# Expert rows of a decoder layer gathered by a list made on chip, in place of a scatter and block loads

## The chip, the cores and the metric

The kernel runs on one core of one Trainium2 chip. The time is device microseconds of one execution, and the figure compared is the median of the runs. All data is float32.

## The reference, cut to what matters

One layer of a decoder: 512 tokens of width 1024, an attention part, then a mixture of 16 experts with a gated residual. The expert part is what the change touches:

```python
def grouped_moe(u, w_router, w1, w3, w2):
    xt = u.reshape(B * T, D)                                  # 512 x 1024
    aff = softmax(xt @ w_router)                              # 16 experts in 4 groups
    g_sel = argmax(group_score)                               # best group by its two best affinities
    top_w, top_i = top_k(where(in_group, aff, -1.0), 2)       # two experts of that group
    ...
    for e in range(16):
        h = silu(xt @ w1[e]) * (xt @ w3[e])                   # 1024 -> 512
        y = y + gate[:, e:e + 1] * (h @ w2[e])                # 512 -> 1024
```

Each token needs only its two experts, so the kernel computes 1024 rows in all.

## The kernel before, in words

Everything up to the router is left as it is. Its last part, L1189 to L1208, projects the attention output in pieces and makes `norm_x`, the normalised rows: ACT's `x_hat(i)` (L703) writes a tile of 128 tokens and counts `r_xh`; with them the columns are already in the order in which the four 256-wide parts of a row are wanted.

**Routing.** DVE finds the two experts of each token (L1224 to L1244), TensorE counts tokens per expert with small products (L1721), and DVE turns the counts into blocks of `BT` = 32 rows, at least `MIN_BLOCKS` = 2 for each expert, and into `posf`, the place of each of a token's two rows among all blocks (L1249 to L1257). For the inputs of the reference the experts take 3, 2, 3, 2, 2, 3, 2, 3, 3, 2, 2, 3, 3, 4, 3 and 2 blocks, 42 in all.

**Rows to blocks.** The DRAM buffer `xs` (`expert_rows`) is zeroed early (L454), and once `idx` is there GpSimd scatters `norm_x` into it with eight indirect DMAs (L833), 128 rows of 4 KB each. The rows of a block are then loaded from it, 32 partitions by 1024, by ACT's queue (`xg_load`, L726) into one of two buffers, and DVE copies them to `xg` (`rows_in`, L1286). The first `NH` = 3 blocks do without: DVE writes a table `pick` of ones and zeros (L1261), and TensorE multiplies it with `norm_x` (`pick_rows`, L1734), which gives each block as 128 partitions by 256, four parts of a row over each other.

**A block.** TensorE's `stage_of(g, ...)` (L1784) is `inner` (L1766: 64 matmul instructions, the two first matrices), `xg_T` (L1756: eight transposes of the next block's rows), and `outer` (L1777: 32 instructions, the third matrix, for the block before). ACT does the SiLU (L730), DVE the product with it (L1315), the scaling of the transposed rows (L1296, L1299), the copy of the block after next (L1286), a transpose (L1303) and the output scaling (`rows_out`, L1308). `inner(g)` waits at its last eighth for `m_cp`, the copy of block g + 1; the next `inner` waits for `m_xv`, its scaled rows. GpSimd stores the block's output rows into `xs` (`store_rows`, L843).

**Weights.** SP's queue loads three matrices of 2 MB for each expert (`load_matrix`, L468). There are four buffers for the pairs of first matrices and three for the third ones. The order is written out by hand (L474 to L513): for expert e the third matrix of e + 3 after the last block's `outer`, then the two first ones of e + 4. At the start experts 0 and 1 and two matrices of expert 2 are there early; (3, 1), (3, 0) and (2, 0), named as (expert, matrix), wait for the scatter (L490 to L500), since `norm_x` and the routing tables lie where they go. (4, 0) and (4, 1) follow when the third block's `inner` is done.

**End.** After the last `outer` the last rows are stored, GpSimd gathers both rows of each token from `xs` (L855), DVE weighs and adds them (L1369, L1374), and SP stores the output (L518).

Of the kernel before, what the change touches and what calls it, by code (L numbers as in the profile page):

```python
# [13 lines left out]
P = 128  # L14
# [34 lines left out]
NH = 3  # L49
N_SCAT = 6  # L50
# [3 lines left out]
N_ROWS = -(-(MAXB + 2) * BT // P) * P  # L54


def decoder_layer(nc, x, c, w_router, ada_w, ada_b, norm1_g, norm2_g, w_in, w_out, nsa_q_gain, nsa_k_gain,
# [6 lines left out]
    with ctx:  # L64
# [42 lines left out]
        def view(at, *shape):  # L107
# [3 lines left out]
            v = att[:, at[0]:at[0] + n]  # L111
# [7 lines left out]
        at = [0]  # L119
# [42 lines left out]
        at = [5120]  # L162
        aff, first, second, gate, cand, aff2 = [view(at, TT, NE) for _ in range(6)]
        both = att[:, 5120 + TT * NE:5120 + 3 * TT * NE].rearrange("p (b x) -> p b x", b=2)
# [10 lines left out]
        assert at[0] <= 6144  # L175
# [3 lines left out]
        zeros_f = sb("zeros_f", [P, 2 * P])  # L179
# [4 lines left out]
        xg = rowbuf[0:BT, 0:D]  # L184
        xg_in = [rowbuf[(1 + n) * BT:(2 + n) * BT, 0:D] for n in range(2)]
# [21 lines left out]
        first_xg = zeros_f[:, :]  # L207
        place = sb("place", [P, NH * BT])
# [128 lines left out]
        s_rows = sem("s_rows")  # L337
        s_ys = [sem(f"s_ys{n}") for n in range(2)]
        s_scat = sem("s_scat")
        s_scat_end = sem("s_scat_end")  # L340
# [69 lines left out]
        def _(sp):  # L410
# [72 lines left out]
            sp.dma_start(mod_rows_col[:], mod_dram.rearrange("(s a) (b k) -> (a b) s k", s=2, k=KD)).then_inc(s_mr, 16)  # L483
            for i in range(TT - 1):
# [37 lines left out]
        def _(act):  # L522
# [209 lines left out]
            def block_of_rows(g, n):  # L732
                silu_of(g)
                act.wait_ge(m_cp, g + 3)
                xg_load(g + 4, n)

            for g in range(2):
                silu_of(g)
            act.wait_ge(s_scat, 16 * N_SCAT)
            act.wait_ge(s_scat_end, 16 * (2 * TT - N_SCAT))  # L740
            xg_load(3, 1)
            xg_load(4, 0)
            act.wait_ge(m_cp, 4)
            xg_load(5, 1)
# [9 lines left out]
            act.wait_ge(s_xg[1], pairs * 16)  # L754
            nc.scalar.activation(cond_e[:], cond_e[:], ACT.Copy)

        @block.gpsimd
        def _(pool):
# [9 lines left out]
            nc.gpsimd.iota(place[:], pattern=[[1, NH * BT]], base=0, channel_multiplier=0, allow_small_or_imprecise_dtypes=True)  # L768
# [44 lines left out]
            nc.gpsimd.memset(zeros_f[:], 0.0).then_inc(t_const, 1)  # L813
# [14 lines left out]
            pool.wait_ge(s_rows, 16 * N_ZERO)  # L828
            pool.wait_ge(r_xh, TT)
# [1009 lines left out]
```

## Time and profile before

| What | Value |
|---|---|
| median of 3 runs | 689.77 us (687.86 to 694.4) |
| the profiled execution's own time | 687.71 us |
| its span in the profile | 686.0 us |
| TensorE busy | 605.6 us, 88% |
| DVE, ACT, GpSimd busy | 58%, 23%, 10% |
| mean granted TensorE clock | 0.96 |

The span is what the profile shows from the first to the last instruction; 1.7 us of the execution lie around it. Busy times are shares of that span. A matmul's end is modelled, and in the last two thirds of the expert part TensorE is busy nearly without a gap, while the sixteen DMA engines are too.

### The profile page before, as it was taken

To read this page: it belongs to the slowest core of one execution; us is meant where nothing else is said; L and a number is where in the kernel's file an instruction comes from. 1 tells how busy PE (TensorE), PEld (TensorE's weight loads), DVE (VectorE), ACT (ScalarE), POOL (GpSimd) and SP (SyncE) were. 2 spreads that over 40 slices of the span, in tenths; PEclk is the share of its full clock that TensorE was granted. 3 is DMA by queue.
4 is the path that set the end of the run, shared out by engine and by line. 5 is a ranking of instruction groups with operands and counts; after the bars stand their busy time and mean duration, and the time that the engine had idled before them with its cause. 6 is when DMAs were issued, how large, how long until landed. Compare 5 with 4: busy or idle time off the path is not lost.

```text
span 686.0 us, 15994 instructions
## 1 busy us (share of the span) xinstructions
PE 605.6 (88%) x6493; PEld 378.1 (55%) x6493; DVE 400.6 (58%) x1018; ACT 157.6 (23%) x405; POOL 71.2 (10%) x121
## 2 busy tenths in 40 slices
PE   0999999998898899779999989999999789999940
PEld 0654474577666566555447646666655445656620
DVE  4746709324489999962335645666655544666636
ACT  5201000103566667851335000000000000000000
POOL 6010000008100000000000400000000000000022
PEclk9999999999899999999999989999999989999975
DMA  8995936144699400019403899999999999999828
GB/s 312 389 400 210 358 117 245 62 126 132 204 332 216 140 1 1 1 57 427 193 32 149 342 360 387 390 387 379 380 380 391 391 406 399 376 370 383 302 62 330
DMA packets 43973, 180.39 MB, mean 263 GB/s; under 512 B 5714, under 2 KB 22698, under 8 KB 35722
## 3 DMA queue, kind: packets, MB, share of 16 engines
q1 hardware_dynamic: 35328, 157.11, 62.1%
q0 software_dynamic: 4352, 13.91, 5.5%
q10 hardware_dynamic: 4236, 8.55, 3.7%
q8 instruction: 44, 0.72, 0.4%
q14 instruction: 13, 0.11, 0.0%
HBM read 156.74 MB, written 22.81 MB: 262 GB/s over the span
## 4 chain that ended last, share of the span: by engine, by line
PE 36%; DMA 17%; DVE 1%; POOL 1%; issue 1%; POOLq 0%; DVEq 0%; ACT 0%
DMA pool_sb<-in_moe_w 14%; PE score L1766 13%; PE score L1632 8%; PE score L1777 8%; PE bank L1756 2%; PE bank L1386 1%; DMA pool_sb<-expert_rows,idx 1%; DMA pool_sb<-expert_rows 1%; POOL pool_sb L855 1%; PE bank L1734 1%; PE bank L1670 1%; DVE gate_row L1308 0%; PE bank L1681 0%; DMA expert_rows<-gate_row 0%; PE bank L1577 0%
## 5 line engine op out<-in xcount | busy, mean ns | idle before, releaser
L1766 PE MATMUL score<-pool_sb 128*32 128x256 f32 x2688 | 157.8, 388 | 10.8 <-DMA pool_sb<-in_moe_w 8.4
L1766 PEld LDWEIGHTS score<-pool_sb 128*32 128x32 f32 x2688 | 89.0, 112 | 72.5 <-issue 14.7
L1411 PE MATMUL bank<-pool_sb 128*128 128x512 f32 (+2 forms) x256 | 84.6, 491 | 0.7 <-DVE pool_sb L932 0.5
L1777 PE MATMUL score<-pool_sb 128*32 128x256 f32 x1312 | 81.0, 388 | 1.7 <-DMA pool_sb<-in_moe_w 1.4
L730 ACT ACTIVATE pool_sb<-score 128x128 f32<-128x128 f32 x41 | 11.4, 278 | 259.7 <-PE score L1766 250.0
L1308 DVE TENSOR_TENSOR gate_row<-score,gate_part 32x256 f32<-32x256 f32 x164 | 67.9, 414 | 3.7 <-PE score L1777 1.4
L1411 PEld LDWEIGHTS bank<-pool_sb 128*128 128x128 f32 x256 | 48.5, 190 | 36.1 <-issue 31.6
L1315 DVE TENSOR_TENSOR pool_sb<-pool_sb,score 128x128 f32<-128x128 f32 x42 | 15.9, 378 | 88.2 <-ACT pool_sb L730 86.4
L1632 PE MATMUL score<-pool_sb 128*128 128x512 f32 (+1 forms) x144 | 57.1, 549 | 0.0
L1777 PEld LDWEIGHTS score<-pool_sb 128*32 128x32 f32 x1312 | 39.1, 111 | 25.5 <-DMA pool_sb<-in_moe_w 2.0
L636 ACT ACTIVATE pool_sb<-pool_sb,nmax 128x128 f32<-128x128 f32 (+2 forms) x96 | 50.0, 526 | 4.6 <-DVE nmax L1036 4.5
L843 POOL DMA_DIRECT2D expert_rows<-gate_row x42 | 20.7, 492 | 248.6 <-DVE gate_row L1308 248.6
L1554 PE MATMUL bank<-ident,pool_sb 128*128 128x128 f32 x216 | 29.7, 280 | 15.6 <-DVE pool_sb L1068 15.4
L1632 PEld LDWEIGHTS score<-pool_sb 128*128 128x128 f32 x144 | 26.6, 190 | 24.9 <-issue 24.2
L1554 PEld LDWEIGHTS bank<-ident,pool_sb 128*128 128x128 f32 x216 | 23.1, 141 | 29.8 <-DVE pool_sb L1068 28.3
L925 DVE SCALAR_TENSOR_TENSOR pool_sb<-pool_sb,cond 128x2048 f32<-128x2048 f32 x16 | 37.5, 2347 | 1.5 <-DMA pool_sb<-in_ada_w 0.7
L1541 PE MATMUL score<-pool_sb 64*128 64x256 f32 (+3 forms) x192 | 32.9, 458 | 0.9 <-ACT pool_sb L621 0.9
L1036 DVE CUSTOM_DVE_ANT_0 pool_sb<-score,pool_sb 128x128 f32<-128x128 f32 (+2 forms) x64 | 27.9, 487 | 9.3 <-PE score L1541 9.1
L1756 PEld LDWEIGHTS bank<-ident,pool_sb 32*128 32x128 f32 x328 | 23.8, 139 | 17.1 <-issue 17.1
L1286 DVE COPY pool_sb<-pool_sb 32x1024 f32<-32x1024 f32 x40 | 27.3, 681 | 6.8 <-DMA pool_sb<-expert_rows 5.6
L1068 DVE TENSOR_SCALAR pool_sb<-pool_sb,fac 128x128 f32<-128x128 f32 (+2 forms) x96 | 29.4, 366 | 1.0
L1577 PE MATMUL bank<-pool_sb 128*64 128x128 f32 x432 | 29.6, 279 | 0.0
(274 smaller groups left out, 692.1 us busy)
## 6 DMA issues: line engine op xcount, KB each, us to landing
pool_sb<-in_moe_w SPq DMA_DIRECT2D x48, 2048.0 KB, 30.6
pool_sb<-in_ada_w SPq DMA_DIRECT2D x16, 1024.0 KB, 7.0
expert_rows<-zeros_f SPq DMA_DIRECT2D x17, 512.0 KB, 6.3
expert_rows<-gate_row POOLq DMA_DIRECT2D x42, 128.0 KB, 7.0
pool_sb<-expert_rows ACTq DMA_DIRECT2D x41, 128.0 KB, 6.9
pool_sb<-in_ada_w SPq DMA_DIRECT2D x8, 640.0 KB, 12.6
pool_sb<-in_w_out SPq DMA_DIRECT2D x4, 1024.0 KB, 16.5
pool_sb<-in_ada_w SPq DMA_DIRECT2D x8, 384.0 KB, 8.6
```

The costliest lines, as they stand in the source:

```text
L636: m = nc.scalar.activation(p, p, ACT.Exp, scale=-1.0, bias=nmax[:, u % 3, b, n:n + 1], accum_out=sums[:, u % 3, b, n:n + 1])
L925: nc.vector.scalar_tensor_tensor(out=acc[:, g % 2, :], in0=stage[:, n % 3, :], scalar=cond[:, k:k + 1], in1=acc[:, g % 2, :], op0=ALU.mult ...
L1068: m = nc.vector.tensor_scalar(p, p, fac[:, b, n:n + 1], None, ALU.mult)
L1308: m = nc.vector.tensor_tensor(y[:, h * DN:(h + 1) * DN], banks[bank][rows, 0:DN], gate2_part[rows, :], ALU.mult)
L1411: m = nc.tensor.matmul(pj_bank(g, i)[:, 0:n], featT[:, k, i * P:(i + 1) * P], w_stage[:, g % 3, k, 0:n], start=(k == 0), stop=(k == KD - 1))
L1541: m = nc.tensor.matmul(banks[2 * (u % 2) + b][:, off:off + w], qT[half, slot_of(t), q * P:(q + 1) * P], kT[half, r, k0:k0 + w], start=True ...
L1554: m = nc.tensor.transpose(banks[4 + b][:, at0:at0 + P], probs[:, u % 3, b, at0:at0 + P], ident[:])
L1577: m = nc.tensor.matmul(O[b * DH:(b + 1) * DH, q * P:(q + 1) * P], proj[:, k0 // P + n, V_COL[r] + b * DH:V_COL[r] + (b + 1) * DH], probsT[ ...
L1632: m = nc.tensor.matmul(banks[2 * (j % 2) + g][:, 0:n], featT[:, 4 * g + k, i * P:(i + 1) * P], w_out_sb[:, 4 * g + k, c0:c0 + n], start=(k ...
L1756: m = nc.tensor.transpose(banks[4][:, k * BT:(k + 1) * BT], xg[:, k * P:(k + 1) * P], ident[0:BT, 0:BT])
L1766: mm = nc.tensor.matmul(banks[0][h * BT:(h + 1) * BT, 0:2 * HB], xgT[:, k, :], w[:, :, h, :], start=(k == 0), stop=(k == KD - 1))
L1777: mm = nc.tensor.matmul(y[h * BT:(h + 1) * BT, 0:DN], h_of[:, c * BT:(c + 1) * BT], exp_w2[e % 3][:, c, h * DN:(h + 1) * DN], start=(c == ...
```

## The change

The scatter, the loads of blocks and their eight transposes go. `norm_x` is stored to DRAM in token order (`xh_dram`, four DMAs of 512 KB). A list `row_list`, 128 rows by one column for each block, is made on chip: for each place in a block it says which 1 KB quarter row of `xh_dram` each partition takes. It comes from a product of two one-hot tables (`rows_hot` times the token number, `blocks_hot`). GpSimd then gathers each block from the third on with one indirect DMA of 128 rows of 1 KB, in the layout 128 by 256 that so far only the first blocks had, so that all blocks need two transposes. `NH` is 2. The routing tables move to a tile of their own, and (3, 0) waits for the router's products alone.

```diff
-NH = 3
-N_SCAT = 6
+NH = 2
+N_LIST = MAXB + 3
...
-        xg = rowbuf[0:BT, 0:D]
-        xg_in = [rowbuf[(1 + n) * BT:(2 + n) * BT, 0:D] for n in range(2)]
+        xg = rowbuf[:, 0:DN]
+        xg_in = [rowbuf[:, (1 + n) * DN:(2 + n) * DN] for n in range(2)]
...
+        routing = sb("routing", [P, 576])
+        xh_tiles = xh_dram.rearrange("(i p) d -> p i d", p=P)
+        xh_parts = xh_dram.rearrange("t (c n) -> (t c) n", c=NT)
...
@@ block.sync @@
             for i in range(TT - 1):
                 store_x2(i)
+                store_x_hat(sp, i)
             sp.wait_ge(o_pj, NS)
             load_matrix(1, 0)
+            store_x2(TT - 1)
             load_matrix(1, 1)
-            store_x2(TT - 1)
-            sp.wait_ge(s_scat, 16 * N_SCAT)
+            sp.wait_ge(o_x, NS)
+            sp.wait_ge(r_lt, TT + 1)
+            load_matrix(3, 0)
             sp.wait_ge(r_xh, TT)
             sp.wait_ge(r_tr, NS)
             sp.wait_ge(s_keep, 16 * TT)
             load_matrix(3, 1)
-            sp.wait_ge(m_ye, 1)
-            load_matrix(3, 0)
-            sp.wait_ge(s_scat, 16 * N_SCAT)
-            sp.wait_ge(s_scat_end, 16 * (2 * TT - N_SCAT))
+            sp.wait_ge(s_xh, 16 * TT)
             sp.wait_ge(r_prod, 4)
             load_matrix(2, 0)
@@ block.scalar @@
+            act.wait_ge(r_xh, TT)
+            act.dma_start(xh_tiles[:, TT - 1, :], norm_x[:, TT - 1, :]).then_inc(s_xh, 16)
...
             with act.Fori(1, pairs - 1) as m:
                 for n in range(2):
-                    block_of_rows(m * 2 + n, n)
+                    silu_of(m * 2 + n)
@@ block.gpsimd @@
-            for n in range(2 * TT):
-                if n % TT == 0:
-                    pool.wait_ge(t_idx, n // TT + 1)
-                pool.indirect_dma_start(out=xs, out_offset=bass.IndirectOffsetOnAxis(ap=idx[:, n:n + 1], axis=0),
-                                        in_=norm_x[:, n % TT, :], in_offset=None).then_inc(s_scat if n < N_SCAT else s_scat_end, 16)
-
+            def gather_rows(g, n):
+                nc.gpsimd.tensor_copy(rows_now[:, n:n + 1], row_list[:, bass.ds(g, 1)]).then_inc(r_now, 1)
+                pool.wait_ge(r_now, g - NH + 1)
+                nc.gpsimd.tensor_tensor(scr[:, 0:TT], ones[:, 0:TT], ones[:, 0:TT], ALU.mult)
+                pool.indirect_dma_start(out=xg_in[n], out_offset=None, in_=xh_parts,
+                                        in_offset=bass.IndirectOffsetOnAxis(ap=rows_now[:, n:n + 1], axis=0)).then_inc(s_xg[n], 16)
+
+            pool.wait_ge(s_xh, 16 * TT)
+            pool.wait_ge(r_hot, 3)
+            for g in range(NH, NH + 2):
+                gather_rows(g, g % 2)
+            pool.wait_ge(m_cp, 3)
+            gather_rows(NH + 2, 0)
...
             with pool.Fori(0, pairs - 1) as m:
                 for n in range(2):
+                    pool.wait_ge(m_cp, m * 2 + n + 4)
+                    gather_rows(m * 2 + n + 5, 1 - n)
                     store_rows(y_sb[n], m * 2 + n, n)
@@ block.vector @@
-            nc.vector.tensor_copy(idx[:], posf).then_inc(t_idx, 2)
...
+            ch(nc.vector.tensor_scalar(block_at[:], posf, 1.0 / BT, 0.5 / BT - 0.5, ALU.mult, ALU.add))
+            ch(nc.vector.tensor_scalar(block_at[:], block_at[:], ROUND, None, ALU.add))
+            ch(nc.vector.tensor_scalar(block_at[:], block_at[:], -ROUND, None, ALU.add))
+            ch(nc.vector.scalar_tensor_tensor(out=row_at[:], in0=block_at[:], scalar=-float(BT), in1=posf, op0=ALU.mult, op1=ALU.add))
+            ch(nc.vector.tensor_tensor(rows_hot[:], place[:, 0:BT].unsqueeze(1).broadcast_to([P, 2 * TT, BT]),
+                                       row_at[:].unsqueeze(2).broadcast_to([P, 2 * TT, BT]), ALU.is_equal))
+            nc.vector.tensor_tensor(rows_hot[:], rows_hot[:], token[:].unsqueeze(2).broadcast_to([P, 2 * TT, BT]), ALU.mult).then_inc(r_hot, 1)
...
             first_rows(0)
+            nc.vector.tensor_tensor(blocks_hot[:], place[:].unsqueeze(1).broadcast_to([P, 2 * TT, N_LIST]),
+                                    block_at[:].unsqueeze(2).broadcast_to([P, 2 * TT, N_LIST]), ALU.is_equal).then_inc(r_hot, 1)
             xg_T(0)
+            dve.wait_ge(r_prod, 4)
+            ch(nc.vector.tensor_scalar(listf[:], banks[3][:, 0:N_LIST], part[:], None, ALU.add))
+            nc.vector.tensor_copy(row_list[:], listf[:]).then_inc(r_hot, 1)
...
+            first_rows(1)
+            hidden(0)
+            rows_in(2, 0, 1)
+            hmid_T(0)
             ch(nc.vector.tensor_reduce(lsum, aff, AX.X, ALU.add))
...
@@ block.tensor @@
-            def first_T():
+            def xg_T():
                 for q in range(2):
-                    m = nc.tensor.transpose(banks[4][:, q * P:(q + 1) * P], first_xg[:, q * P:(q + 1) * P], ident[:])
+                    m = nc.tensor.transpose(banks[4][:, q * P:(q + 1) * P], xg[:, q * P:(q + 1) * P], ident[:])
                 m.then_inc(m_xt, 1)
...
-            pick_rows(1, 0)
             pe.wait_ge(m_cp, 1)
-            first_T()
-            for i in range(1, TT):
+            xg_T()
+            for i in range(TT):
                 m = pick_rows(1, i)
             m.then_inc(r_prod, 1)
...
+            pe.wait_ge(r_hot, 2)
+            for n in range(2 * TT):
+                for k in range(NT):
+                    m = nc.tensor.matmul(banks[3][k * BT:(k + 1) * BT, 0:N_LIST], rows_hot[:, n, :], blocks_hot[:, n, :],
+                                         start=(n == 0), stop=(n == 2 * TT - 1))
+            m.then_inc(r_prod, 1)
...
             inner(0, 0)
-            first_T()
-            for i in range(TT):
-                m = pick_rows(2, i)
-            m.then_inc(r_prod, 1)
+            xg_T()
```

Left out: the same renaming in `first_rows` and in DVE's `xg_T` (one form for all blocks), `pick` 64 instead of 96 columns wide, small constants of GpSimd and DVE made before the expert part, the two instructions that wait for the last loads, and the six operations of `pairs` and `block_start` (L1265 to L1270), which now stand behind `row_list`. The thirteen small operations that make the weights `wab` (L1323 to L1333) and `idx` stood behind the first block's `xg_T` and now stand behind `hmid_T(0)`.

## Rows read from the trace of the kernel before

**Rows 1.** Stretches: busy us of PE, PEld, DVE, ACT, POOL; clock, DMA share, GB/s.
```profile
395.00:411.00 16.00, 13.48 (x196) 7.74 (x192) 6.22 (x16) 0.56 (x2) 0.57 (x1) 0.83 1.02 360
...
411.00:440.00 29.00, 29.00 (x501) 17.44 (x496) 17.33 (x43) 1.39 (x5) 2.48 (x5) 0.97 1.00 385
...
530.00:560.00 30.00, 25.05 (x410) 14.18 (x399) 14.23 (x35) 0.86 (x4) 1.96 (x4) 0.89 1.01 400
...
640.00:657.00 17.00, 17.00 (x305) 10.28 (x300) 9.75 (x24) 0.93 (x4) 1.47 (x3) 1.00 0.53 197
```

**Rows 2.** The chain, one block in the steady part: start us, us, what.
```profile
447.40 3.45 PE score L1766 x64
450.86 0.61 PE bank L1756 x8
451.47 1.86 PE score L1777 x32
```

**Rows 3.** PE timeline: the two long weight waits, and the last outer.
```profile
548.34 5.64 PE L1766 MATMUL score<-pool_sb 128*32 128x256 f32 x64 [4.95 <-DMA pool_sb<-in_moe_w]
...
565.82 5.35 PE L1766 MATMUL score<-pool_sb 128*32 128x256 f32 x64 [3.43 <-DMA pool_sb<-in_moe_w]
...
657.18 1.91 PE L1777 MATMUL bank<-pool_sb 128*32 128x256 f32 x32
```

**Rows 4.** DMA issues: what, queue, count, KB each, median us to landing.
```profile
pool_sb<-in_moe_w SPq DMA_DIRECT2D x48, 2048.0 KB, 30.6
expert_rows<-gate_row POOLq DMA_DIRECT2D x42, 128.0 KB, 7.0
pool_sb<-expert_rows ACTq DMA_DIRECT2D x41, 128.0 KB, 6.9
...
expert_rows<-pool_sb,idx POOLq DMA_INDIRECT x8, 5.1
pool_sb<-expert_rows,idx POOLq DMA_INDIRECT x8, 6.3
```

**Rows 5.** SP's timeline, the first weight loads of the expert part.
```profile
394.61 1.06 SPq L468 DMA_DIRECT2D pool_sb<-in_moe_w  x2
397.12 0.33 SPq L468 DMA_DIRECT2D pool_sb<-in_moe_w  x1
406.35 0.81 SPq L468 DMA_DIRECT2D pool_sb<-in_moe_w  x2
```

**Rows 6.** Timeline of all engines, the first blocks.
```profile
385.79 0.42 DVE L1277 COPY zeros_f<-bank 128x256 f32<-128x256 f32 x1 [0.57 <-PE bank L1734]
...
386.27 0.44 PE L1740 MATMUL bank<-ident,zeros_f 128*128 128x128 f32 x2 [0.18 <-DVE zeros_f L1277]
...
391.66 0.28 ACT L730 ACTIVATE pool_sb<-score 128x128 f32<-128x128 f32 x1 [13.42 <-PE score L1766]
391.83 0.95 POOL L833 DMA_INDIRECT expert_rows<-pool_sb,idx  x1 [0.30 <-issue]
...
391.89 1.93 PE L1734 MATMUL bank<-pool_sb 128*32 128x256 f32 x32
...
392.64 0.42 DVE L1299 TENSOR_TENSOR pool_sb<-pool_sb,mod_rows_col 128x256 f32<-128x256 f32 x1
...
393.86 3.66 PE L1766 MATMUL score<-pool_sb 128*32 128x256 f32 x64
...
404.67 0.68 DVE L1286 COPY pool_sb<-pool_sb 32x1024 f32<-32x1024 f32 x1 [5.61 <-DMA pool_sb<-expert_rows]
```

**Rows 7.** Timeline: a product of 32-column weights with 128 columns.
```profile
365.45 0.16 PEld L1681 LDWEIGHTS bank<-pool_sb,wr_scaled 128*32 128x32 f32 x8 [0.33 <-issue]
```

**Rows 8.** POOL timeline, the first gather at the end.
```profile
663.87 0.19 POOL L852 TENSOR_TENSOR rstd<-rstd 128x4 f32<-128x4 f32 x1 [1.81 <-DMA expert_rows<-gate_row]
664.63 1.02 POOL L855 DMA_INDIRECT pool_sb<-expert_rows,idx  x1 [0.56 <-issue]
```

**Rows 9.** DMA queues at 69.2 to 71.6 us: packets, MB, share of 16 engines.
```profile
q1 hardware_dynamic: 91, 0.75, 74.2%
q10 hardware_dynamic: 105, 0.22, 24.7%
```

**Rows 10.** DMA queues at 178 to 200 us, zeros in packets of 1 KB.
```profile
q1 hardware_dynamic: 7436, 7.39, 101.4%
```

More of the change, by code:

```diff
@@ L206, in decoder_layer @@
         ssq2h = sb("ssq2h", [P, 3, TT])
-        first_xg = zeros_f[:, :]
-        place = sb("place", [P, NH * BT])
+        place = sb("place", [P, N_LIST])
+        token = sb("token", [P, 2 * TT])
+        part = sb("part", [P, 1])
+        block_at = sb("block_at", [P, 2 * TT])
+        row_at = sb("row_at", [P, 2 * TT])
+        rows_hot = sb("rows_hot", [P, 2 * TT, BT])
+        blocks_hot = sb("blocks_hot", [P, 2 * TT, N_LIST])
+        listf = sb("listf", [P, N_LIST])
+        row_list = sb("row_list", [P, N_LIST], U32)
+        rows_now = sb("rows_now", [P, 2], U32)
+        xh_dram = nc.dram_tensor("normalised_rows", (T, D), F32, kind="Internal").ap()
+        xh_tiles = xh_dram.rearrange("(i p) d -> p i d", p=P)
+        xh_parts = xh_dram.rearrange("t (c n) -> (t c) n", c=NT)
         x2_dram = nc.dram_tensor("rows_after_attention", (T, D), F32, kind="Internal").ap().rearrange("(i p) d -> p i d", p=P)
@@ L753, in _ @@
             silu_of(last)
-            act.wait_ge(s_xg[1], pairs * 16)
-            nc.scalar.activation(cond_e[:], cond_e[:], ACT.Copy)
         @block.gpsimd
@@ L849, in _ @@
                 store_rows(y_last[n], pairs * 2 + (n - 2), n)
+            for n in range(2):
+                pool.wait_ge(s_xg[n], (pairs + 1 - n) * 16)
+            pool.wait_ge(t_idx, 1)
             for n in range(2):
@@ L1145, in _ @@
             chain.n = 0
+            dve.wait_ge(t_const, 3)
+            chain(nc.vector.tensor_scalar(part[:], token[:, 0:1], 1.0 / P, 0.5 / BT - 0.5, ALU.mult, ALU.add), r_chain, 0)
+            chain(nc.vector.tensor_scalar(part[:], part[:], ROUND, None, ALU.add), r_chain, 0)
+            chain(nc.vector.tensor_scalar(part[:], part[:], -ROUND, None, ALU.add), r_chain, 0)
             def residual1(j):
@@ L1257, in _ @@
             ch(nc.vector.tensor_reduce(posf, both.rearrange("p b (i e) -> p (b i) e", e=NE), AX.X, ALU.add))
-            nc.vector.tensor_copy(idx[:], posf).then_inc(t_idx, 2)
-            dve.wait_ge(s_rows, 16 * N_ZERO)
+            dve.wait_ge(r_lt, TT + 1)
             for i in range(TT):
-                ch(nc.vector.tensor_scalar(pick[:, i, :], place[:], posf[:, i:i + 1], None, ALU.is_equal))
-                nc.vector.scalar_tensor_tensor(out=pick[:, i, :], in0=place[:], scalar=posf[:, TT + i:TT + i + 1], in1=pick[:, i, :],
+                ch(nc.vector.tensor_scalar(pick[:, i, :], place[:, 0:NH * BT], posf[:, i:i + 1], None, ALU.is_equal))
+                nc.vector.scalar_tensor_tensor(out=pick[:, i, :], in0=place[:, 0:NH * BT], scalar=posf[:, TT + i:TT + i + 1], in1=pick[:, i, :],
@@ L1270, in _ @@
-            nc.vector.tensor_copy(block_start[:], gsf[0:1, :]).then_inc(t_gs, 1)
-            def first_rows(g):
-                dve.wait_ge(r_prod, g + 2)
-                if g < 2:
-                    if g > 0:
-                        dve.wait_ge(m_xt, g)
-                    m = nc.vector.tensor_copy(first_xg, banks[5 + g][:, 0:DN])
-                else:
-                    for c in range(NT):
-                        m = nc.vector.tensor_copy(xg[:, c * DN:(c + 1) * DN], banks[5 + g][c * BT:(c + 1) * BT, 0:DN])
-                m.then_inc(m_cp, 1)
+            ch(nc.vector.tensor_scalar(block_at[:], posf, 1.0 / BT, 0.5 / BT - 0.5, ALU.mult, ALU.add))
@@ L1333, in _ @@
                 ch(nc.vector.tensor_tensor(wab[:, b * TT:(b + 1) * TT], wab[:, b * TT:(b + 1) * TT], wsum, ALU.mult))
-            nc.vector.memset(y_last[0][0:1, 0:1], 0.0).then_inc(m_ye, 1)
-            first_rows(1)
-            hidden(0)
-            first_rows(2)
-            hmid_T(0)
+            nc.vector.tensor_copy(idx[:], posf).then_inc(t_idx, 1)
             dve.wait_ge(t_gs, 1)
@@ L1746, in _ @@
             m.then_inc(r_prod, 1)
-            pick_rows(1, 0)
             pe.wait_ge(m_cp, 1)
-            first_T()
-            for i in range(1, TT):
+            xg_T()
+            for i in range(TT):
                 m = pick_rows(1, i)
             m.then_inc(r_prod, 1)
-            def xg_T():
-                for k in range(KD):
-                    m = nc.tensor.transpose(banks[4][:, k * BT:(k + 1) * BT], xg[:, k * P:(k + 1) * P], ident[0:BT, 0:BT])
-                m.then_inc(m_xt, 1)
+            pe.wait_ge(r_hot, 2)
[4 more added lines that the diff above has]
+            m.then_inc(r_prod, 1)
             def inner(e, g):
```

85 lines of the change are left out of this document (36 added, 49 removed).

## The prediction

> **What bounds the kernel now.** I read the table of stretches first. From 411 us on the DMA engines are busy all the time at 385 GB/s, also where TensorE is not (530 to 560 us: TensorE 25.05 of 30 us, DMA share 1.01), and they fall to 0.53 only after 640 us [rows 1]. So the expert part has two bounds close together. The chain shows the first: a block costs TensorE 3.45 + 0.61 + 1.86 = 5.93 us [rows 2]. The timeline shows the second: two `inner` start late, at 548.34 after 4.95 us and at 565.82 after 3.43 us, both on a weight [rows 3]; by the blocks per expert these are blocks 25 and 27, the first ones of experts 10 and 11. After that TensorE does 15 blocks nearly without a wait and ends at 657.18 + 1.91 = 659.1 us [rows 3]. What lies behind it (last stores, the gathers at the end, the output), 687.7 - 659.1 = 28.6 us of the execution's own time, isn't changed.
>
> The DMA list shows that a 2 MB weight takes 30.6 us from issue to landing [rows 4]. At the pace of the stream, 2.097 MB at 385 GB/s less the rows (0.262 MB per 5.93 us, 44 GB/s), one takes 2.097/0.341 = 6.15 us, so about five are queued at any time. The blocks' own loads land in 6.9 us and stores in 7.0 [rows 4]. A gain of TensorE alone would be eaten by these weights; what counts is when the stream of weights starts.
>
> **The change, part by part.**
>
> *The block's transposes.* Eight small ones cost 0.61 us in the chain [rows 2]; two of 128 x 128 cost 0.44 with the wait before them [rows 6], in a full pipeline between 0.2 and 0.44. I take 0.25: a block is 5.56 us. Behind it, DVE's copy shrinks from 1024 to 256 columns (0.68 us for 1024, 0.42 for 256 out of PSUM [rows 6]), which is hidden either way. Does the next `inner` then wait for its scaled rows? In the start one `inner` ends at 391.6, the SiLU starts at 391.66 and the second scaling ends at 392.64 + 0.42 = 393.06 [rows 6]: 1.5 us, against 0.25 + 1.86 = 2.1 on TensorE. Still hidden.
>
> *The start.* The path to the first copy at 385.79 [rows 6] is paced by TensorE's own products, so narrower tables give nothing. Copy and transposes end at 386.7 as before; then `pick_rows(1)` is whole, 32 instructions, 1.9 us [rows 6], to 388.6. The list product comes next on TensorE: 64 instructions of 32-column weights and 67 columns. The nearest row loads 8 such weights in 0.16 us [rows 7], so 64 take 1.3; by columns they take 3.45 x 67/256 = 0.9 [rows 2]. At 0.4 us for a group of 8 with its latency it would be 3. I take 1.5: `inner(0)` starts at 390.1 and not at 388.1, and ends at 393.6. The products of block 2 (1.93 us [rows 6]) that covered the scaling are gone, so it shows: 1.5 us, and `inner(1)` starts at 395.1 (before 393.86 [rows 6]).
>
> DVE has the list at about 390.7. On GpSimd a gather needs a copy and a dummy product (0.19 each by the small operation there, and 0.56 before the gather starts [rows 8]): it starts at 391.8. Its landing is the large unknown. The same instruction with 128 rows of 4 KB lands in 6.3 us, the scatter in 5.1 [rows 4], neither beside weights; the plain loads and stores beside weights take 6.9 and 7.0 [rows 4]. Below I bound it by 5 and 12; I take 7, and 8 in the steady part. So block 2's rows are there at 398.8, the copy at 399.1, and `inner(1)`, whose last eighth is due at 398.1, waits 1 us. `outer(0)` ends at about 401.8. Meanwhile DVE does the thirteen small operations, now behind `hmid_T(0)`, some 0.2 us each, 2.7 us, and only then the product and scaling for block 1's hidden rows, 1.2 us: `inner(2)` starts near 403.3 and ends near 406.7. That is where it ended before: (4, 0) went out at 406.35 [rows 5], because there block 3's rows came from the scatter only at 404.67 [rows 6]. Between the bounds it is 404 to 411.
>
> *The weights at the start.* Before, (3, 1) and (3, 0) went out at 394.61 and (2, 0) at 397.12 [rows 5], behind the scatter's 4.2 MB, whose last issue is at 391.83 [rows 6]. With three weights in front, (4, 0) started moving at about 396 + 3 x 6.15 = 414.5. Now (3, 0) waits for the router alone, (3, 1) for the stored rows. From 369.6 the queue holds (1, 0), (1, 1), (3, 0), (3, 1) and 1.5 MB of rows, 9.9 MB, 26 us: done by 397. (2, 0) goes out after the list product, near 391, and is done by 403. So (4, 0) no longer waits for the engines but for `inner(2)`: it moves at 406.7 + 1 = 407.7. The stream of the other 37 weights starts 6.8 us earlier, between 3 and 9 by the bounds above.
>
> *The bytes.* A block's rows are the same 128 KB in and out. In packets of 1 KB the zeros moved 7.39 MB at a share of 101.4% of 22 us, 337 GB/s [rows 10] against 385 in the stage: a block's 128 KB costs 0.39 instead of 0.34 us of all engines, nothing. The 2 MB of normalised rows go out before 385 us, where the scatter was not yet, and 4.2 MB of scatter go.
>
> *The sum.* The stream is the bound, so the landings count. (11, 1) landed at 565.8 [rows 3] and lands at 559.0. (13, 1) is six weights on: 559.0 + 6 x 6.15 = 595.9. From it nine blocks are left: 9 x 5.56 + 1.9 = 51.9, end 647.8. The same from expert 11: 559.0 + 15 x 5.56 + 1.9 = 644.3; from expert 15: 559.0 + 12 x 6.15 + 2 x 5.56 + 1.9 = 645.8. The latest is 647.8, 11.3 us before 659.1. The execution's 687.7 becomes 676.4. The median of the runs shown is 2 us above that execution, which I take as scatter of the runs; I say **677 us**. The bounds of the start and of the transposes make it 671 to 682.
>
> **What speaks against it: the gathers' turns.** Each block's rows used to be 32 packets of 4 KB, two for each of 16 engines, and one for the semaphore. Gathered they are eight of 1 KB. Where ACT's queue and SP's were both full, 91 packets of 8 KB and 105 of 2 KB went by in the same 2.4 us [rows 9]: the engines took them in turn, one by one, whatever their size. If GpSimd's queue is served so, each 1 KB row waits for a 16 KB weight packet (16.4 KB at 385/16 = 24 GB/s per engine: 0.68 us). No row shows GpSimd's 1 KB packets beside weights, only its 4 KB ones, whose 7.0 us fit two turns and one for the semaphore.
>
> The Trainium skill ("DMA: Bandwidth & Descriptors", "SWDGE vs HWDGE vs iDMA") says that the engines change queues only at packet boundaries, and that GpSimd's packets preferably hold up to 4096 bytes. By it four rows of 1 KB could share a packet and a gather would take two turns, as the loads did, so that nothing of the forecast changes; without such packing it is the first rival. No row decides between them.
>
> **The rivals.**
>
> *Turns, one for each row (slower).* A block then has on GpSimd's queue 8 + 1 turns for the gather and 2 + 1 for the store: 12 x 0.68 = 8.2 us at most, about 8 in practice. It decides as soon as weights are queued, since 8 is above both 5.56 and the 6.15 x 37/39 = 5.8 us of weights per block. The weights, 37 x 8 = 296 packets per engine, give turns for 296/12 = 24.7 blocks at 8 us; then they are through, run ahead and stop at full buffers, and the other 14.3 blocks take 5.56. That is 277 us for the 39 blocks from block 3 on, which starts at about 409 + 3 (the first gathers are late too): 689, 30 us after 659.1. As weights also move while no row is waiting, some of it comes back: 22 to 30 us, **712 to 718**, I say 714. For it: the alternation in rows 9. Against it: it was seen between the two hardware queues only, and the 128 rows at the end are issued and landed like any other DMA [rows 4].
>
> *The stream gives little.* The gathers land in 10 to 12 us at first, `inner(2)` ends at 411 and (4, 0) moves at 412, 2.5 us earlier than now; in the steady part a gather is asked for when the block two before is copied, and must be back in 2 x 5.56 = 11.1 us with 1.1 us on GpSimd and 0.3 of copy in it, so above 9.7 us it starts to add waits in the experts with three blocks. 687.7 - 2.5 - 3 or so: **683**, within 1%.
>
> *The stream does not bind.* If the DMA engines keep up (clock gaps of TensorE gave them their waits), each block gives its 0.37 us: 39 x 0.37 = 14.4 us, and block 3 starts at 408.9 in place of 410.8: **671**. Against it: the DMA share of 1.00 over 411 to 440 us already [rows 1].
>
> *The change doesn't do what it says*: the list could be late and all rows with it. Its price is that of the second rival.
>
> **How the numbers follow.** The forecast has 0.49, the turns 0.33, little gain 0.12, the full gain 0.06. About 1% is what a measurement of this kernel can tell from no change (683 to 697). Faster 0.55, same 0.12, slower 0.33. The likeliest case's own range is 671 to 682; with the first rival at 712 to 718 the range that leaves out 2 in 10 is 670 to 715.
>
> **What would show it.** Right: the chain's transposes at 0.2 to 0.3 us a block; L468 out before 385 us twice more and (4, 0) at about 407; DMA share still 1.0 from 411 to 630; three to five weight waits of 2 to 7 us on TensorE, at experts 10, 11 and 13, some 20 us in all; gathers landing in 7 to 9 us; the last `outer` at 648. Wrong, the first rival: gathers landing in 10 us or more, `inner` waiting at its last eighth for DVE's copy and `outer` for DVE, no wait for weights, DMA share at 0.85, weights landing in 6 to 20 us instead of 30. Wrong, the second: `inner(2)` ending after 410 us. A list product above 3 us or a clock below 0.9 between 390 and 410 us would spoil the start.

## The result and the profile after

The changed kernel takes **663.3 us** (median of four runs, 662.42 to 665.88); the kernel before, run beside it, takes 690.6 (687.86 to 694.4). The ratio is 0.961, interval 0.955 to 0.966. It is faster, as forecast, but by 27 us instead of 13, and it lies below my range of 670 to 715.

The profiled execution took 662.42 us: span 660.6, mean clock 0.978. Its table of stretches has the columns of [rows 1]:

```profile
395.00:411.00 16.00, 14.21 (x242) 7.91 (x246) 9.58 (x35) 0.83 (x3) 5.22 (x11) 1.00 0.64 233
411.00:440.00 29.00, 29.00 (x509) 16.45 (x502) 16.40 (x47) 1.39 (x5) 10.35 (x21) 1.00 0.96 387
440.00:470.00 30.00, 30.00 (x526) 17.06 (x522) 17.00 (x48) 1.39 (x5) 10.01 (x21) 1.00 1.01 419
...
530.00:560.00 30.00, 26.33 (x429) 14.62 (x424) 14.30 (x40) 1.11 (x4) 8.82 (x18) 0.94 1.01 420
560.00:590.00 30.00, 30.00 (x526) 16.89 (x514) 16.34 (x47) 1.39 (x5) 10.22 (x21) 1.00 1.01 423
```

Read the last two numbers of each row. The DMA engines are as busy as before (1.01) but move about 420 GB/s from 440 to 590 us, where the kernel before moved 383 to 400. I had read the 1.00 of [rows 1] as a limit in bytes. It is a share of time, and each byte now takes less of it.

The chain shows one block, to be laid beside [rows 2]:

```profile
501.57 3.45 PE score L1782 x64
505.02 0.37 PE bank L1756 x2
505.39 1.91 PE score L1793 x32
```

The transposes cost 0.37 us, not 0.25, so a block is 5.69 us. TensorE's timeline, beside [rows 3], keeps one long wait for a weight, and its last `outer` starts 25 us earlier:

```profile
545.05 5.35 PE L1782 MATMUL score<-pool_sb 128*32 128x256 f32 x64 [3.67 <-DMA pool_sb<-in_moe_w]
...
632.06 1.91 PE L1793 MATMUL bank<-pool_sb 128*32 128x256 f32 x32
```

The `inner` of 5.35 us behind the wait ran partly at half clock: the granted clock over these 5.35 us is 0.68, after 3.67 us in which TensorE did nothing, and 3.64 us is its usual time. So this wait cost its own length and 1.7 us more.

The start came out near the forecast. TensorE's and SP's timelines show the list product (1.1 us, forecast 1.5), the three first `inner`, and (4, 0) and (4, 1) going out at 402.72:

```profile
384.50 1.14 PE L1771 MATMUL score<-blocks_hot,rows_hot 128*32 128x67 f32 x64
385.45 4.28 PE L1782 MATMUL score<-pool_sb 128*32 128x256 f32 x64
...
391.22 3.76 PE L1782 MATMUL score<-pool_sb 128*32 128x256 f32 x64 [1.11 <-DVE pool_sb L1304]
...
399.00 3.66 PE L1782 MATMUL score<-pool_sb 128*32 128x256 f32 x64 [1.79 <-DVE pool_sb L1304]
```
```profile
402.72 1.02 SPq L479 DMA_DIRECT2D pool_sb<-in_moe_w  x2
```

(4, 0) had left at 406.35 [rows 5] and I had it ready at 406.7. But 3.9 us of this difference lie ahead of the expert part, which isn't changed: from 150 to 200 us the granted clock (the number before the last two) is 0.90 in the profile of before and 1.00 after. Run f below shows that this is chance.

```profile
150.00:200.00 50.00, 42.22 (x345) 32.47 (x345) 28.94 (x84) 22.01 (x53) 16.45 (x13) 0.90 0.70 224
```
```profile
150.00:200.00 50.00, 41.71 (x382) 32.79 (x382) 32.12 (x97) 25.36 (x65) 16.57 (x14) 1.00 0.74 236
```

The first gather is issued at 387.19 and its rows are copied at 393.99, so it lands in at most 6.8 us (7 forecast):

```profile
387.19 1.10 POOL L835 DMA_INDIRECT pool_sb<-normalised_rows,rows_now  x1 [0.36 <-issue]
...
393.99 0.29 DVE L1295 COPY pool_sb<-pool_sb 128x256 f32<-128x256 f32 x1 [2.83 <-DMA pool_sb<-normalised_rows,rows_now]
```

How it travels stands in the list of DMA queues from 440 to 600 us:

```profile
DMA packets 6759, 67.37 MB, mean 421 GB/s; under 512 B 1335, under 2 KB 1335, under 8 KB 3085
## 3 DMA queue, kind: packets, MB, share of 16 engines
q1 hardware_dynamic: 4119, 59.92, 88.9%
q0 software_dynamic: 2623, 7.17, 11.4%
```

The packets between 2 and 8 KB number 3085 - 1335 = 1750. In this stretch 27 stores and 28 gathers went out (by the issues of the same list), 55 transfers, so there are 32 for each: a gather of 128 rows of 1 KB is 32 packets of 4 KB, four rows in one. The weights' bytes on q1 make 59.92 MB / 16384 = 3657 packets in 88.9% of 16 x 160 us: **0.62 us** for 16 KB. The same sum from the list of before gives **0.67**, 8% more:

```profile
DMA packets 6174, 62.07 MB, mean 388 GB/s; under 512 B 1204, under 2 KB 1204, under 8 KB 2780
...
q1 hardware_dynamic: 3795, 55.33, 89.0%
q10 hardware_dynamic: 1180, 3.20, 6.1%
q0 software_dynamic: 1182, 3.26, 5.2%
```

### The profile page after: what moved, and what is told of

It reads as the page before. It is cut to its first block, busy times and chain, and to the rows that moved or that the text cites. A ratio compares the mean times of both kernels' runs of the same rounds, so it can differ in the third digit from the quotient of the medians.

```text
span 660.6 us, 15641 instructions
## 1 busy us (share of the span) xinstructions
PE 585.3 (89%) x6279; PEld 358.2 (54%) x6279; DVE 381.2 (58%) x1027; ACT 157.4 (24%) x404; POOL 125.7 (19%) x243
## 4 chain that ended last, share of the span: by engine, by line
PE 43%; DMA 8%; DVE 2%; POOL 1%; issue 1%; POOLq 0%; DVEq 0%; SPq 0%
PE score L1782 18%; PE score L1793 10%; PE score L1648 8%; DMA pool_sb<-in_moe_w 6%; PE bank L1756 2%; PE bank L1402 1%; DMA pool_sb<-expert_rows,idx 1%; DMA pool_sb<-normalised_rows,rows_now 1%; POOL pool_sb L866 1%; PE bank L1750 1%; PE bank L1686 1%; DVE gate_row L1313 1%; PE bank L1697 0%; DMA expert_rows<-gate_row 0%; PE bank L1593 0%
## 5 line engine op out<-in xcount | busy, mean ns | idle before, releaser
L1782 PE MATMUL score<-pool_sb 128*32 128x256 f32 x2688 | 155.2, 382 | 6.6 <-DMA pool_sb<-in_moe_w 3.7
L1782 PEld LDWEIGHTS score<-pool_sb 128*32 128x32 f32 x2688 | 87.8, 111 | 66.3 <-issue 6.3
L1793 PE MATMUL score<-pool_sb 128*32 128x256 f32 x1312 | 79.3, 382 | 0.0
L744 ACT ACTIVATE pool_sb<-score 128x128 f32<-128x128 f32 x41 | 11.4, 277 | 238.6 <-PE score L1782 238.6
L1793 PEld LDWEIGHTS score<-pool_sb 128*32 128x32 f32 x1312 | 38.5, 110 | 28.0 <-issue 6.5
L835 POOL DMA_INDIRECT pool_sb<-normalised_rows,rows_now x43 | 43.4, 1009 | 10.6 <-issue 10.3
L806 POOL TENSOR_TENSOR hrstd<-hrstd,minus_half 128x24 f32<-128x24 f32 (+1 forms) x2 | 14.7, 7360 | 112.5 <-DVE hrstd L971 112.5
L849 POOL DMA_DIRECT2D expert_rows<-gate_row x42 | 23.0, 548 | 59.6 <-DVE gate_row L1313 59.6
L1557 PE MATMUL score<-pool_sb 64*128 64x256 f32 (+3 forms) x192 | 30.6, 432 | 0.9 <-ACT pool_sb L636 0.9
L1427 PE MATMUL score<-pool_sb 128*128 128x512 f32 x64 | 29.7, 623 | 0.0
```

What stands on the lines that cost most here:

```text
L835: pool.indirect_dma_start(out=xg_in[n], out_offset=None, in_=xh_parts, in_offset=bass.IndirectOffsetOnAxis(ap=rows_now[:, n:n + 1], axis=0 ...
L1427: m = nc.tensor.matmul(pj_bank(g, i)[:, 0:n], featT[:, k, i * P:(i + 1) * P], w_stage[:, g % 3, k, 0:n], start=(k == 0), stop=(k == KD - 1))
L1557: m = nc.tensor.matmul(banks[2 * (u % 2) + b][:, off:off + w], qT[half, slot_of(t), q * P:(q + 1) * P], kT[half, r, k0:k0 + w], start=True ...
L1782: mm = nc.tensor.matmul(banks[0][h * BT:(h + 1) * BT, 0:2 * HB], xgT[:, k, :], w[:, :, h, :], start=(k == 0), stop=(k == KD - 1))
L1793: mm = nc.tensor.matmul(y[h * BT:(h + 1) * BT, 0:DN], h_of[:, c * BT:(c + 1) * BT], exp_w2[e % 3][:, c, h * DN:(h + 1) * DN], start=(c == ...
```

## The experiments

What needed a cause was the pace of the weights. What went away in that stretch is q10, ACT's loads of 32 rows of 4 KB into 32 partitions. Two theories: the few partitions disturb the other transfers, or the second hardware queue does. Times are medians. The runs were made in groups, each beside the kernel before; the ratio is to that, with its 95% interval. The kernel before had medians between 685.9 and 690.6 us in these groups, the changed kernel 663.3 and 663.7. a to d form one group, e to h the next, then k to n, then o and p, each group on another chip. Differences within a group are the safest; the intervals reach 2 to 4 us to either side.

**a: GpSimd loads 32 rows of 4 KB.**

```diff
-                pool.indirect_dma_start(out=xg_in[n], out_offset=None, in_=xh_parts, ...
+                pool.dma_start(gate1_row[(2 + n) * BT:(3 + n) * BT, :], xh_dram[n * BT:(n + 1) * BT, :]).then_inc(s_xg[n], 16)
```

> The changed kernel with each block's gather (128 rows of 1 KB) replaced by a plain load on the same GpSimd queue, at the same place and with the same waits: 32 rows of 4 KB into 32 partitions of a buffer that nobody reads (the blocks' rows are then what lies in the copy's source; the output is not computed). Same bytes. Few-partitions theory (transfers that land in only 32 partitions disturb the weights): DMA throughput from 440 to 590 us falls from 420 to 385-395 GB/s, three or more weight waits, time 668 to 674. Hardware-queue theory (what disturbed them was the second hardware queue, ACT's): still 418 to 424 GB/s and 661 to 665.

679.5 us (before 685.9; ratio 0.991, 0.987 to 0.994), 16 us above the changed kernel and more than either theory had. **b: the same by ACT**, behind the SiLU:

```diff
+            def row_load(n):
+                act.dma_start(gate1_row[(2 + n) * BT:(3 + n) * BT, :], xh_dram[n * BT:(n + 1) * BT, :]).then_inc(s_xg[n], 16)
```

> The same plain loads of 32 rows of 4 KB into 32 partitions, but issued by ACT behind the SiLU as the kernel before did; GpSimd issues only the stores. Both theories: throughput 383 to 395 GB/s in 440 to 590 us, weight waits of TensorE at experts 10 to 13, time 668 to 676. If it keeps 420 GB/s, both theories fall and the pace came from something else (the weights' places in time, TensorE's waits).

677.2 us (0.988, 0.983 to 0.993). **c: ACT loads 128 rows of 1 KB** with `act.dma_start(xg_in[n], xh_parts[n * P:(n + 1) * P, :])`:

> ACT issues plain loads of 128 rows of 1 KB into 128 partitions (the right buffer, rows of the wrong tokens). Few-partitions theory: 415 to 424 GB/s, time 661 to 666. Hardware-queue theory: 385 to 395 GB/s, 668 to 676. If hardware queues also take 1 KB rows turn by turn between 16 KB weight packets, the loads land in 8 us and more instead of 7 and copies come late: above 680.

665.6 us (0.971, 0.966 to 0.976). **d: the kernel before with wide loads:**

```diff
-                act.dma_start(xg_in[n], xs[bass.ds(g * BT, BT), :]).then_inc(s_xg[n], 16)
+                act.dma_start(rows_wide[:, n * DN:(n + 1) * DN],
+                              xs[bass.ds(g * BT, BT), :].rearrange("r (c n) -> (r c) n", c=NT)).then_inc(s_xg[n], 16)
```

> The kernel before with its row loads turned to 128 partitions of 1 KB in a tile that nobody reads, same queue (ACT), same rows in DRAM, same waits; scatter, eight transposes and the order of the weights untouched (blocks' rows are then stale data). Few-partitions theory: throughput 411 to 560 us rises from 385 to 410-424 GB/s, the weight waits at 548 and 565 (8.4 us) go or shrink below 3, time 7 to 12 us less than before, 678 to 684. Hardware-queue theory: nothing moves, 687 to 692. Turn-by-turn service of 1 KB rows: slower than before, above 695.

**672.6 us** (0.980, 0.977 to 0.983): 13.3 us less by the shape of 128 KB transfers alone, more than I expected. The rows of the stretch from 470 to 500 us, in this order: a, b, c, d.

```profile
470.00:500.00 30.00, 29.91 (x524) 16.92 (x518) 17.11 (x48) 1.39 (x5) 6.97 (x20) 1.00 1.01 384
```
```profile
470.00:500.00 30.00, 30.00 (x520) 16.84 (x512) 16.22 (x46) 1.67 (x6) 4.96 (x16) 1.00 1.01 387
```
```profile
470.00:500.00 30.00, 30.00 (x526) 17.06 (x522) 17.39 (x49) 1.39 (x5) 4.55 (x16) 1.00 1.01 423
```
```profile
470.00:500.00 30.00, 30.00 (x532) 18.14 (x528) 18.88 (x47) 1.39 (x5) 2.45 (x5) 1.00 1.01 422
```

The weights' queue from 440 to 600 us, in the same order:

```profile
q1 hardware_dynamic: 3761, 54.82, 88.7%
```
```profile
q1 hardware_dynamic: 3771, 54.84, 88.8%
```
```profile
q1 hardware_dynamic: 4122, 60.07, 88.4%
```
```profile
q1 hardware_dynamic: 4109, 59.80, 88.2%
```

By the sum above a weight packet takes 0.68 us in a and b and 0.62 in c and d. Which engine issues the loads makes little difference (3 GB/s); the shape in which they land does, and h below tells its two parts apart. The hardware-queue theory falls with a (384 GB/s without ACT's queue) and with c and d (423 and 422 with it). In a the changed kernel's start is kept, and it is 14 us above c and 16 above the changed kernel.

**h: pieces of 1 KB, but in 32 partitions.** As b, with each partition's 4 KB taken from four places (`rearrange("(c r) n -> r c n")` on the source):

> The run with ACT's 32 rows of 4 KB once more, but with the source so ordered that each piece is 1 KB: 128 pieces of 1 KB, four of them in each of 32 partitions. It tells the number of partitions from the size of a piece. If few partitions are what disturbs: 380 to 395 GB/s in 440 to 590 us and 674 to 680, as with 4 KB pieces. If the size of the pieces is: 415 to 424 GB/s and 663 to 668, as with 128 partitions.

676.5 us (0.986, 0.981 to 0.991). From 470 to 500 us:

```profile
470.00:500.00 30.00, 29.26 (x502) 19.56 (x501) 16.26 (x47) 1.39 (x5) 4.55 (x16) 1.00 1.02 398
```

With the same pieces as c it is 398 instead of 423 GB/s: the partitions cost 25 GB/s, and the larger pieces of b another 11. A weight packet takes 0.66 us. Its time is no lower than b's for a second reason: the loads land in 11.5 us, as long as two blocks take, and from 440 to 530 us TensorE waits 3.3 us for DVE. The Trainium skill ("SBUF — State Buffer", "Door 1: The DMA port swizzle") says that DMA reaches the partitions through 16 ports, and that 32 neighbouring partitions lie behind only 8 of them. The longer weight packets would fit that, if the row packets crowd half of the ports and the weight packets meant for these wait; no run here shows a port. A load into 32 partitions that are not neighbours would have tested it, and was not made. That the partitions are the larger part of the cause is shown, why they are is not.

**e: the early weights taken back.**

```diff
-            load_matrix(3, 0)
             sp.wait_ge(r_xh, TT)
...
-            load_matrix(3, 1)
             sp.wait_ge(s_xh, 16 * TT)
-            sp.wait_ge(r_prod, 4)
+            sp.wait_ge(m_h1, 2)
+            load_matrix(3, 0)
+            load_matrix(3, 1)
             load_matrix(2, 0)
```

> The changed kernel with (3, 0), (3, 1) and (2, 0) held back until the second block's inner is done, 394.9 us, as late as they went in the kernel before. Three weights at 5.6 us are then through at 411.6, so (4, 0) moves 8 us later than now. Stream theory (at 420 GB/s it still limits TensorE a little, since one weight wait of 3.7 us is left): that wait grows by about 8 us and others appear, time 668 to 671. Rival (with the faster stream TensorE alone is the bound, the early weights give nothing): 662 to 665.

668.4 us (before 686.1; 0.975, 0.971 to 0.979): **5 us** lost. There are more waits for weights:

```profile
415.84 3.66 PE L1782 MATMUL score<-pool_sb 128*32 128x256 f32 x64 [1.26 <-DMA pool_sb<-in_moe_w]
...
489.64 1.93 PE L1793 MATMUL score<-pool_sb 128*32 128x256 f32 x32 [1.53 <-DMA pool_sb<-in_moe_w]
...
534.38 4.97 PE L1782 MATMUL score<-pool_sb 128*32 128x256 f32 x64 [3.00 <-DMA pool_sb<-in_moe_w]
...
550.42 5.35 PE L1782 MATMUL score<-pool_sb 128*32 128x256 f32 x64 [2.91 <-DMA pool_sb<-in_moe_w]
```

They sum to 8.7 us against 3.7, so the stream theory holds and the rival falls. The 5 us are a balance: without weights beside it the first gather of e is issued at 388.21 and its rows are copied at 391.48, at most 3.3 us later instead of 6.8, and `inner(2)` starts 10.9 us after `inner(0)` instead of 13.6. The early weights thus cost the start 2.7 us and give some 7.7 later.

**f: three more small transposes a block**, `transpose(banks[4][:, 2 * P + q * BT:...], xg[0:BT, 0:P], ...)` for q in 0 to 2:

> The changed kernel with three more small transposes (32 x 128, into unused columns of the bank) ahead of the two of each block, which by the 0.61 us for eight of before is 0.23 us a block, 9 us in all. TensorE theory: a block is 5.92 instead of 5.69, the weight wait of 3.7 us goes, as the weights have more time, and the time rises by 9 less 4 to 6, to 667 to 669. If the stream hides it: below 665. If TensorE were the bound everywhere: 672.

671.2 us (0.978, 0.973 to 0.982), 8 above the changed kernel where I expected 4 to 6. No wait for a weight is left, and a block takes 5.99 us, not 5.92. Two of its four executions took 668.7 and 669.8 us, two 672.7 and 673.7. The profiled one took 673.7, and it has the clock gap of before (150 to 200 us, f):

```profile
150.00:200.00 50.00, 42.30 (x344) 32.41 (x345) 28.77 (x84) 21.82 (x51) 16.62 (x14) 0.90 0.70 225
```

Up to there f is the changed kernel, whose two profiles show 1.00, as do all others taken here but those of g and n (0.93). So the 3.9 us ahead of the expert part are chance. From the start of `inner(0)` to the end of the last `outer`, which leaves them out, f takes 255.0 us and the changed kernel 248.5: the three transposes cost 6.5 us.

**k: scatter, wide loads and two transposes**, that is d with the copies, the transposes and the scaling of the changed kernel, no list, no gather:

```diff
-                nc.vector.tensor_copy(xg, xg_in[n]).then_inc(m_cp, 1)
+                nc.vector.tensor_copy(first_xg, rows_wide[:, n * DN:(n + 1) * DN]).then_inc(m_cp, 1)
...
-                                            banks[4][:, 0:KD * BT].rearrange("p (k r) -> p k r", k=KD),
+                                            banks[4][:, 0:KD * BT].rearrange("p (q r c) -> p c q r", q=2, c=NT),
...
+            xg_T = first_T
```

> The kernel before with its scatter, its three blocks by products and its order of weights, but with the blocks loaded by ACT into 128 partitions of 1 KB and transposed by two instructions; no list, no gather. It computes the reference. Layout theory (the gain is the 128 partitions and the two transposes that they allow): 672.6 of the run with wide loads alone less 39 x 0.24 = 9.4, and 1 to 4 back for weight waits: 664 to 668, which leaves 1 to 5 us for the gather and the early weights. Rival (the gather and the early weights carry a good part): 671 or more.

673.6 us (before 689.3; 0.975, 0.971 to 0.979), above the 664 to 668 of the layout theory, and 10 us above the changed kernel of its group. In its profile DVE was held twice, by 3.5 and 3.8 us, before its first copy and its first scaling, and the profile names no instruction that released it. The same kernel (p), and one with its code shifted (o), were to tell whether that belongs to it:

> The scatter with wide loads and two transposes, with 24 one-column writes put at the start of DVE's program, where it waits for data anyway; they only shift where its later instructions stand. If the two holes of 3 us that DVE showed at the first copies (385 and 389 us, put down to nothing but 'remote') are instructions that arrive late, they move or go: the inner of block 0 starts at 384.3 as in the run with wide loads alone, and the time is 5 to 8 us below the unpadded version of this call, 664 to 668. If the holes stay, they belong to the scatter beside the first products and the time stays at 672 to 675.

> The unpadded version again, to see whether its holes before 392 us come back. If they do: 672 to 675, the inner of block 0 at 390. If they were chance: 664 to 668 in some of its executions.

o took 669.2 (0.972, 0.967 to 0.977) and p 668.8 us (0.973, 0.968 to 0.978), and neither profile has the holes. So the holes don't belong to the kernel, and shifting the code did nothing; what made them, and k's six executions (672.2 to 675.9) slower than p's four (667.3 to 671.7), stays open. Both medians still lie 1 us above the expected 664 to 668. What stays is the wait for block 3's rows in the start, o and p:

```profile
407.66 1.08 PE L1764 MATMUL score<-pool_sb 128*32 128x256 f32 x8 [8.81 <-DVE zeros_f L1285]
```
```profile
404.88 1.05 PE L1761 MATMUL score<-pool_sb 128*32 128x256 f32 x8 [4.86 <-DVE zeros_f L1282]
```

It was 2.38 us in the profile of before and doesn't exist in the changed kernel. The loads are queued behind the scatter and beside the first weights, and on ACT's queue the wide shape lands later (p, DMA issues from 440 to 600 us; 7.0 before):

```profile
DMA packets 9416, 67.47 MB, mean 422 GB/s; under 512 B 1346, under 2 KB 4864, under 8 KB 5736
...
expert_rows<-gate_row POOLq DMA_DIRECT2D x28, 128.0 KB, 6.6
rows_wide<-expert_rows ACTq DMA_DIRECT2D x27, 128.0 KB, 10.8
```

**l, m: the changed kernel again, and a faster version (g, m).** DVE's copy of block 1 goes ahead of the operations on the pairs, and the thirteen small ones are split behind the first two `rows_out` of the start:

```diff
             nc.vector.tensor_copy(row_list[:], listf[:]).then_inc(r_hot, 1)
+            first_rows(1)
...
                 rows_out(y_sb[(g - 1) % 2])
+                weights_of_tokens(g)
```

> A version meant to be faster: DVE's copy of block 1's rows goes ahead of the small operations for the number of pairs, and the thirteen small operations on the tokens' weights go behind the output scaling of the first two blocks of the loop's start, so that nothing stands before the hidden rows of block 1. In the changed kernel inner(0) is held some 0.6 us by that copy and inner(2) 1.8 us by these operations. Expected: inner(2) ends 2 to 2.5 us earlier (at 400.4), (4, 0) with it, time 660.5 to 661.5. If the first gather's landing takes their place, 1 us or less is gained.

> The changed kernel as it is, beside the versions of this call, and for TensorE's clock between 150 and 200 us: a granted clock of 1.00 there in this and most other runs, and 0.90 in a few of any kernel, means that the 3.9 us that the first two profiles differ by before the expert part are chance. Expected 661 to 666, ratio 0.965 to 0.971.

> The version with the small operations moved, again, with more rounds beside the changed kernel: 1 us faster than it (0.5 to 2), since two thirds of the 1.9 us won at the start came back as weight waits in its first run.

g took 662.3 us (0.967, 0.962 to 0.973), above its 660.5 to 661.5. In one group with six executions each, l took 663.7 (0.961, 0.956 to 0.966) and m **661.3** (0.958, 0.954 to 0.963). m is the fastest here, but the intervals overlap. Its profile has the wait of 1.8 us in the start gone, and the one for a weight still there, at 543.5 us with 3.5 us.

**n: stores from 128 partitions**, g with one output scaling of 256 columns and

```diff
-                pool.dma_start(xs[bass.ds(g * BT, BT), :], y).then_inc(s_ys[n], 16)
+                pool.dma_start(xs[bass.ds(g * BT, BT), :].rearrange("r (c n) -> c r n", c=NT), y).then_inc(s_ys[n], 16)
```

> The last version with the output rows of a block kept as 128 partitions of 1 KB too: one output scaling of 256 columns instead of four, and GpSimd's store reads from 128 partitions instead of 32. If transfers that read few partitions disturb the weights as those that write them: throughput from 440 to 590 us rises above 425 GB/s, the weight waits of 5.2 us shrink, 656 to 660. If only writes into few partitions do, or 420 GB/s is what the engines can do: 422 GB/s and 661 to 663 as without. If stores of 1 KB rows are served one by one and land late: DVE waits for a free buffer, above 665.

688.7 us (before 689.3; 0.997, 0.994 to 0.999): 27 us lost, by the third case of the expectation. Its DMA packets from 440 to 600 us, and who waited for the buffer that they read, `gate_row`:

```profile
DMA packets 8575, 65.19 MB, mean 407 GB/s; under 512 B 3467, under 2 KB 3467, under 8 KB 4976
...
q0 software_dynamic: 4528, 6.22, 11.2%
```
```profile
  DVE gate_row L1327: 97.3, 26
  PE score L1795: 26.1, 19
```

The 24 stores and 23 gathers of this stretch would make 48 packets each on q0, 32 of 4 KB and 16 for the semaphore, 2256 in all. There are 4528, so each store brings some 95 small ones more, about six per engine. DVE waits for its buffer 26 times, 97 us in all; TensorE's `outer` behind it waits 26.1 us, which is the loss. Whether reading few partitions disturbs the weights stays open.

**The expert part alone.** From the start of `inner(0)` to the end of the last `outer`, in the profiles, us; what lies ahead, with its chance clock gap, is left out:

| Run | us | What it has |
|---|---|---|
| before | 271.1 | scatter, loads into 32 partitions, eight transposes |
| d | 259.1 | loads into 128 partitions |
| k, o, p | 255.1, 257.9, 252.6 | these, and two transposes |
| after, l | 248.5, 249.6 | list, gather, early weights, two transposes |
| e | 253.5 | as after, weights late |
| a, b, h | 263.7, 262.5, 263.1 | as after, loads into 32 partitions |
| c | 250.4 | as after, ACT's loads into 128 partitions |

## Why the prediction was wrong

*The pace of the stream: the step that failed.* I wrote "2.097/0.341 = 6.15 us" for a weight and kept it under the change. For the kernel before that was near: q1's 55.33 MB in 160 us are 6.06 us for a weight. In the changed kernel q1's 59.92 MB are 5.60. From (4, 0)'s start at 403.7 to the landing of (11, 1) at 545.05 it is 141.3 us; the forecast had 151.3 for the same (407.7 to 559.0), and that is 10 us. By the code's order these are 24 weights, and 24 x 0.46 is 11; a part is lost again around 421 us, where the queue ran empty (DMA share 0.73 from 419 to 422 us). With the faster stream the later weight, (13, 1), bound nothing any more: 3.5 us, the distance of my 647.8 from the 644.3 of expert 11. I had priced the loads by their bytes ("a block's 128 KB costs 0.39 instead of 0.34") and found nothing; runs a to d show that their shape, not their bytes, made each weight packet 8 to 10% longer (0.67 to 0.68 against 0.62 us), and h that it is mostly the number of partitions. Of the three to five waits for weights, some 20 us, that I had named as a sign, one of 3.7 us came. No rival had this: all took the stream as it was, or away.

*The rest of the sum.* The start: 4 us early at (4, 0), of which 3.9 are the chance clock gap of before, so this step was right, and 4 of the 14 us that the execution took less than forecast are luck of the profile that I started from. A block of 5.69 instead of 5.56 costs 15 x 0.13 = 2.0 us behind the last wait, and the half clock there 1.7. Together -4 - 10 - 3.5 + 2.0 + 1.7 = -13.8, which is the last `outer`'s end at 634.0 against my 647.8. The end is 28.4 us (28.6 forecast).

*The early weights.* Right in kind: run e prices them at 5 us, beside my 6.8. That the first gather would land in half the time without them was not in the sum.

*The transposes.* I expected the weights to eat their gain. With the faster stream they don't: in d, with eight transposes, TensorE waits for no weight at all behind its start, so a block's own time counts. Three small transposes more cost 6.5 us (f). From d to o and p two instead of eight gave 3.4 and 3.8 us of time, and 1.2 and 6.5 in the expert part, where the wait for block 3's rows is 8.8 us in o, 4.9 in p and 5.3 in d; k shows no gain in time. How much the old stream would have left of them no run shows.

*The turns.* The first rival's case, at 0.33, fell: the gathers of g land in 7.3 us beside the weights. Four rows share a packet, as the Trainium skill allows ("DMA: Bandwidth & Descriptors", "SWDGE vs HWDGE vs iDMA"). Its mechanism isn't empty: on ACT's hardware queue the 1 KB rows land in 10.8 us (p) and 10.7 (c) instead of 7.0, and n shows what late transfers do once they pass a block's slack. In c it is still 0.7 us inside the 11.4 of two blocks, and c is 2 us above the changed kernel. (The 22 to 30 us of this rival make 710 to 718 us from 687.7, not 712 to 718.)

*The gather itself.* Layout alone: 13.3 us (d). With two transposes: 669 us (o, p), or 673.6 (k). The list, the gather and the early weights give the rest: 5.5 and 5.9 us by p and o, 10 by k, 4 to 9 in the expert part. e takes 5 of it with the early weights alone. The gather's own part is then mainly that it lets the weights go early, and that it carries 1 KB rows without their turns; no run has it alone.

## What to carry to other kernels

A DMA share of 1.0 says that time is used up, not bytes: look at GB/s and at the time of one packet, and ask which small transfer beside the stream lengthens it. Here 128 KB per block into 32 partitions made the 16 KB packets of a stream 8% longer; spreading the same bytes over 128 partitions gave half of the whole gain with two changed lines, and would have been the first thing to try. Then look at how late the spread rows land on their queue: on ACT's each 1 KB piece was a packet of its own, and they took 10.8 us instead of 7.0. And compare the granted clock stretch by stretch ahead of the changed part before a difference is explained: here it was worth 3.9 us by chance.

## What was not expected of the hardware

- The same 128 KB per block, into 32 or 128 partitions: 384 and 387 against 422 and 423 GB/s for all transfers, at a share of 1.01 both times.
- 128 rows of 1 KB are 32 packets of 4 KB in a GpSimd gather, and separate packets on ACT's queue: p has 4864 - 1346 = 3518 packets of that size in 160 us for its 27 loads of 128 rows, and a landing of 10.8 us.
- A store from 128 partitions whose DRAM side is cut in 1 KB pieces (n) brings some 95 packets under 512 bytes with it, and the kernel lost 27 us.
- The first gather, 128 rows of 1 KB, lands in at most 6.8 us beside the weights and in at most 3.3 us without them (e).
